# A hybrid attention, gating and retrieval layer on one core: all 128 chunks of one table turned during one projection

## The chip, the cores and the metric

The kernel runs on one core of one Trainium2 chip. The metric is the device time of one execution in microseconds (us), as the median of several runs. The profiled execution is another run of the same program, and its span runs from its first to its last instruction. In the rows below PE is the matrix engine, PEld its weight loads, DVE, ACT and POOL are the vector, scalar and GpSimd engines, and SP is the engine that here only issues transfers. A name with a q behind it (SPq, ACTq, POOLq) is the row of a transfer that this engine issued.

## What is computed

One layer of an encoder over 1024 tokens of width 1024, all in float32. The parts that matter here:

```python
h = rms_norm(x, g_pre_mix) * (1.0 + sc1) + sh1
p = h @ w_in                                  # the input projection, 56 column tiles of 128
q, k, v, z, gates = jnp.split(p, SPLITS, axis=-1)
o = diff_attention(q, k, v, lam)              # -> y_attn
sg = spatial_gating(jax.nn.gelu(z), ...)      # z = (u, v): u * mixed(layer_norm(v)) -> y_gmlp
gate_a, gate_g = jnp.split(jax.nn.sigmoid(gates), 2, axis=-1)
mix = (gate_a * y_attn + gate_g * y_gmlp) @ w_out
x = x + gt1 * rms_norm(mix, g_post_mix)
y = peer(rms_norm(x, g_pre_ffn) * (1.0 + sc2) + sh2, ...)

def peer(h, w_q, sub_keys, exp_u, exp_v):     # 16384 experts of one neuron each
    ...                                       # idx: for each token 8 heads x 16 experts
    u = exp_u[ib]
    a = jax.nn.gelu(jnp.einsum('td,ted->te', xb, u)) * gb
    return jnp.einsum('te,ted->td', a, exp_v[ib])
```

## The kernel before

The layer is a row of stages with a barrier of all engines between them. A matrix product is made of three products of rounded parts (`product3`: high by high, high by low, low by high), so that a tile of 128 output columns for 1024 tokens costs 48 matmuls of 128x512: two halves of the tokens, eight blocks of the inner dimension, three products each.

The method `projection` is the loop that several stages share. It goes over the column tiles of a weight. For each tile SP loads 512 KB of the weight (`raw`), ACT rounds it to the high part (L456), DVE makes the low part (L488), PE does the 48 matmuls (L382 to L384) into one of two accumulators, and the stage's own functions `act_out` and `dve_out` empty the accumulator. Weights and accumulators are double buffered.

Four stages matter:

- the **front** projection, 32 tiles of `w_in`, called in `gmlp_and_gates`. It has three stretches: 8 tiles of u (ACT applies gelu and stores 512 KB to `gelu_u_scratch`), 8 tiles of the other half of z (ACT applies gelu into SBUF, nothing is stored), and 16 tiles of gates (ACT applies the sigmoid and stores 512 KB to `gate_scratch`). In the gate tiles DVE also multiplies and sums pieces of the modulation matrix, and POOL loads 1024 KB of it for each tile (`gates_ada`, L1047), as soon as one of two buffers is free. The first two of the 16 pieces are loaded at the start of the stage.
- the **attn** and **spat** projections, 8 tiles each, with no row chunks;
- the **out** projection, 8 tiles of `w_out`, whose accumulator ACT squares (L1424) and copies (L1425), while DVE sums the squares.

Beside its own work a projection can turn **row chunks**. The table `peer_u` lies in memory with its inner dimension first, in 128 chunks of 128 experts. The last stage wants to fetch single experts as rows, so each chunk is loaded (512 KB), transposed by PE in eight 128x128 blocks, copied out of PSUM by ACT and stored as rows in `u_rows_scratch` (512 KB). How many chunks a tile turns, and from which chunk on, is the argument `rows=(per_tile, row_base)`. The chunks have two buffers on the way in (`r_in`), two in PSUM (`r_ps`) and two on the way out (`r_out`). The places in a tile come from `rows_at`: with three chunks they stand ahead of the 3rd, 9th and 14th of the 16 blocks of three matmuls, with four ahead of the 3rd, 7th, 11th and 15th. The three engines go like this:

```python
# SP, for each chunk n of tile j (after the weight of tile j + 2)
sp.wait_ge(r_turned, whole(n + 1))            # chunk n - 2 has been turned: r_in is free
sp.dma_start(r_in[:, slot], ... "peer_uT" ...).then_inc(r_loaded[slot], 16)
# PE, turn_rows
pe.wait_ge(r_loaded[slot], n * 8 + (16 - 8 * slot))
pe.wait_ge(r_copied, n + 1)                   # chunk n - 2 has left PSUM
for k in range(KT): last = pe.transpose(r_ps[slot][...], r_in[...], self.ident[:])
# ACT, empty, ahead of the tile's own output
act.wait_ge(r_turned, n + 3)
act.wait_ge(r_stored[slot], n * 8 + (16 - 8 * slot))   # chunk n - 2 has been stored
act.activation(r_out[:, slot], r_ps[slot], ACT.Copy).then_inc(r_copied, 1)
act.dma_start(self.u_rows[...], r_out[:, slot]).then_inc(r_stored[slot], 16)
```

All three engines work in order, so a chunk that is late holds what stands behind it on its engine. The first is L434 and L435, the second L550 to L554, the third L461 to L466. In the kernel before, the front projection turns three chunks per tile (96) and the out projection four (32).

Of the kernel before, what the change touches and what calls it, by code (L numbers as in the profile page):

```python
# [29 lines left out]
KT = D // P  # L30
# [23 lines left out]
Q0, K0, V0, ZU0, ZV0, GA0, GG0 = 0, 8, 16, 24, 32, 40, 48  # L54


class Layer:
# [925 lines left out]
    def gmlp_and_gates(self, h_hi, h_lo):  # L983
# [4 lines left out]
        nc, a, ps = self.nc, self.a, self.psum  # L988
        GATES = 2 * KT
        TILES = 2 * KT + GATES  # L990
# [9 lines left out]
        with ExitStack() as c:  # L1000
# [4 lines left out]
            with ExitStack() as p:  # L1005
                buf = self.sb(p, "front_buf", [P, 2, T])
                ada = self.sb(p, "gates_ada", [P, 2, 2, D])
                products = self.sb(p, "gates_products", [P, 2, 2, D])
                cb = self.sb(p, "gates_cb", [P, D])

                def to_scratch(func, dst, begin, made_before):

                    def act_out(act, j, s, acc, emptied):
                        own = j - begin

                        act.wait_ge(stored[s], (own + made_before) * 8 + (16 - 8 * s))
                        act.activation(buf[:, s], acc, func).then_inc(emptied, 1)

                        act.wait_ge(emptied, j + 3)
                        act.dma_start(dst[bass.ds(own, 1)].rearrange("o p t -> (o p) t"), buf[:, s]).then_inc(stored[s], 16)  # L1020
                    return act_out

                def zv_act_out(act, j, s, acc, emptied):
                    act.activation(zv[:, bass.ds(j - KT, 1)].rearrange("p o t -> p (o t)"), acc, ACT.Gelu_apprx_tanh).then_inc(emptied, 1)

                def zv_dve_out(dve, j, s, acc, emptied):

                    dve.wait_ge(emptied, j + 3)
                    dve.wait_ge(summed, j - KT + 1)
                    dve.tensor_tensor(total[:], total[:], zv[:, bass.ds(j - KT, 1)].rearrange("p o t -> p (o t)"), ALU.add).then_inc(summed, 1)  # L1030

                def gates_dve_out(dve, j, s, acc, emptied):
                    own = j - 2 * KT
                    dve.wait_ge(ada_loaded[s], own * 8 + (16 - 8 * s))

                    dve.wait_ge(dotted, own + 1)
                    dve.tensor_tensor(products[:, s], ada[:, s], cb[:].unsqueeze(1).to_broadcast([P, 2, D]), ALU.mult).then_inc(multiplied, 1)
                    dve.wait_ge(multiplied, own + 3)
                    dve.tensor_reduce(self.mod[:, bass.ds(own * 2 + MADE, 2)], products[:, s], AXX, ALU.add).then_inc(dotted, 1)

                def pool_program(pool, emptied):
                    with pool.Fori(0, GATES // 2) as it:
                        at = [pool.snap(it * 4 + (2 * s + MADE)) for s in range(2)]
                        for s in range(2):

                            pool.wait_ge(multiplied, it * 2 + (s + 1))
                            pool.dma_start(ada[:, s], a["w_adaT"][:, bass.ds(at[s], 2), :]).then_inc(ada_loaded[s], 16)  # L1047
                with nc.Block() as block:
                    @block.sync
                    def _(sp):  # L1050
                        sp.dma_start(cb[:], a["c"].to_broadcast([P, D])).then_inc(c_loaded, 16)
                        sp.dma_start(w[:].rearrange("q g p -> q (g p)"), a["w_spatial"]).then_inc(tables, 16)
                        sp.dma_start(bias[:].rearrange("q g p -> q (g p)"), a["b_spatial"].to_broadcast([P, KT * P])).then_inc(tables, 16)

                    @block.scalar
                    def _(act):
                        act.wait_ge(c_loaded, 16)
                        act.activation(cb[:], cb[:], ACT.Silu).then_inc(chain, 1)

                    @block.tensor  # L1060
                    def _(pe):
                        for s in range(2):
                            pe.sem_inc(stored[s], 16)

                    @block.vector
                    def _(dve):
                        dve.sem_inc(multiplied, 2)
                        dve.sem_inc(dotted, 2)
                        dve.memset(total[:], 0.0).then_inc(summed, 1)
                self.projection("front", a["w_in"], ZU0, h_hi, h_lo, TILES, pool_program=pool_program, rows=(3, 0), segments=[  # L1070
                    (0, KT, to_scratch(ACT.Gelu_apprx_tanh, self.u_scr, 0, 0), None),
                    (KT, 2 * KT, zv_act_out, zv_dve_out),
                    (2 * KT, TILES, to_scratch(ACT.Sigmoid, self.gate_scr, 2 * KT, KT), gates_dve_out)])
                with nc.Block() as block:
                    @block.sync
                    def _(sp):
                        for s in range(2):
                            sp.wait_ge(stored[s], 16 * ((KT + GATES) // 2 + 1))
# [335 lines left out]
    def out_projection(self, wide, m_hi, m_lo, total):  # L1414

        squared = self.sem("out_squared")
        summed = self.sem("out_summed")
        with ExitStack() as c:
            sq = self.sb(c, "out_sq", [P, 2, T])

            def act_out(act, j, s, acc, emptied):

                act.wait_ge(summed, j + 1)
                act.activation(sq[:, s], acc, ACT.Square).then_inc(squared, 1)  # L1424
                act.activation(wide[:, bass.ds(j, 1)].rearrange("p o t -> p (o t)"), acc, ACT.Copy).then_inc(emptied, 1)  # L1425

            def dve_out(dve, j, s, acc, emptied):
                dve.wait_ge(squared, j + 1)
                dve.wait_ge(summed, j + 2)
                dve.tensor_tensor(total[:], total[:], sq[:, s], ALU.add).then_inc(summed, 1)  # L1430
            with self.nc.Block() as block:
                @block.vector
                def _(dve):
                    dve.memset(total[:], 0.0).then_inc(summed, 1)
                    dve.sem_inc(summed, 1)
            self.projection("out", self.a["w_out"], 0, m_hi, m_lo, KT, act_out=act_out, dve_out=dve_out, rows=(4, 3 * 4 * KT))


    def add_normed(self, name, y, coef, base_dram, x1, dst_dram, total=None, squares_too=False):
# [1161 lines left out]
```

## Time and profile before

| | |
|---|---|
| median of 3 runs | 4668.48 us |
| lowest and highest run | 4663.53 and 4678.07 us |
| span of the profiled execution | 4674.6 us |
| PE busy | 3809.2 us, 81% of the span |
| DVE busy | 2888.6 us, 62% |
| ACT busy | 1496.4 us, 32% |
| POOL busy | 1266.7 us, 27% |
| read from and written to memory | 901.56 MB and 146.28 MB |

The stages follow each other with barriers, so what a change does in one stage shows in the length of that stage and moves all that follows. The shares of the whole span say little about a single stage. The front projection lasts from about 937 to 1397 us of the span, the out projection from about 1778 to 1903 us.

### The profile page before, as it was taken

To read this page: it belongs to the slowest core of one execution; us is meant where nothing else is said; L and a number is where in the kernel's file an instruction comes from. 1 tells how busy PE (TensorE), PEld (TensorE's weight loads), DVE (VectorE), ACT (ScalarE), POOL (GpSimd) and SP (SyncE) were. 2 spreads that over 40 slices of the span, in tenths; PEclk is the share of its full clock that TensorE was granted. 3 is DMA by queue.
4 is the path that set the end of the run, shared out by engine and by line. 5 is a ranking of instruction groups with operands and counts; after the bars stand their busy time and mean duration, and the time that the engine had idled before them with its cause. 6 is when DMAs were issued, how large, how long until landed. Compare 5 with 4: busy or idle time off the path is not lost. (4 is left out here: it accounts for less than half of the span.)

```text
span 4674.6 us, 50598 instructions
## 1 busy us (share of the span) xinstructions
PE 3809.2 (81%) x17580; PEld 2788.3 (60%) x17580; DVE 2888.6 (62%) x5552; ACT 1496.4 (32%) x2161; POOL 1266.7 (27%) x1080
## 2 busy tenths in 40 slices
PE   1889999699995898698666654389999999999996
PEld 1656666478775677587555543256666666665553
DVE  5666766401334431479677876877777777776665
ACT  3444444243433213411465561022222222221211
POOL 0000000000001000000000224667677767675442
PEclk9989999699995899699888877689999999999998
DMA  3000000087982226410245669899999999999996
GB/s 133 25 19 25 23 18 16 28 300 276 349 324 108 90 90 244 167 48 18 91 126 159 207 193 307 283 385 401 391 396 399 399 388 405 395 403 376 369 364 248
DMA packets 383399, 1050.26 MB, mean 225 GB/s; under 512 B 33264, under 2 KB 102256, under 8 KB 380016
## 3 DMA queue, kind: packets, MB, share of 16 engines
q0 software_dynamic: 153504, 567.35, 32.2%
q1 hardware_dynamic: 180960, 338.52, 21.1%
q10 hardware_dynamic: 48752, 142.10, 7.8%
q8 instruction: 96, 1.57, 0.1%
q14 instruction: 87, 0.71, 0.0%
HBM read 901.56 MB, written 146.28 MB: 224 GB/s over the span
## 5 line engine op out<-in xcount | busy, mean ns | idle before, releaser
L2280 POOL DMA_INDIRECT ex_v_rows<-peer_v_dram,expert_of x512 | 625.5, 1222 | 293.4 <-PE psum L2509 147.3
L2412 DVE TENSOR_TENSOR y<-y,psum 128x512 f32<-128x512 f32 x512 | 349.8, 683 | 379.8 <-PE psum L384 377.2
L382 PE MATMUL psum<-in_hi 128*128 128x512 f32 x1024 | 422.0, 412 | 67.0 <-ACT sc_gelu_t L2029 52.2
L2272 POOL DMA_INDIRECT ex_u_rows<-u_rows_scratch,expert_at x352 | 396.1, 1125 | 268.7 <-DVE dots L2405 176.7
L2405 DVE CUSTOM_DVE_ANT_1 ex_u_rows<-ex_u_rows,y 128x1024 f32<-128x1024 f32 x352 | 429.8, 1222 | 57.1 <-DMA ex_u_rows<-u_rows_scratch,expert_at 41.5
L382 PE MATMUL psum<-in_hi,v_hi 128*128 128x512 f32 x1024 | 430.6, 421 | 0.2 <-issue 0.2
L383 PE MATMUL psum<-in_lo,in_hi 128*128 128x512 f32 x1024 | 408.5, 399 | 0.0
L384 PE MATMUL psum<-in_hi,in_lo 128*128 128x512 f32 x1024 | 406.8, 397 | 0.0
L383 PE MATMUL psum<-in_lo,v_hi 128*128 128x512 f32 x1024 | 406.0, 396 | 0.0
L384 PE MATMUL psum<-in_hi,v_lo 128*128 128x512 f32 x1024 | 404.8, 395 | 0.0
L1047 POOL DMA_DIRECT2D gates_ada<-w_adaT_dram x16 | 8.7, 541 | 1363.2 <-PEq L532 931.4
L2509 PE MATMUL psum<-ex_v_rows,ex_spread 128*32 128x512 f32 x2048 | 283.3, 626 | 94.1 <-DMA ex_v_rows<-peer_v_dram,expert_of 93.0
L382 PEld LDWEIGHTS psum<-in_hi,v_hi 128*128 128x128 f32 x1024 | 194.9, 190 | 223.2 <-issue 125.0
L2130 PE MATMUL psum<-sc_first,sc_second 128*128 128x128 f32 x1024 | 169.3, 333 | 175.3 <-DVE sc_second L1957 175.3
L2323 ACT ACTIVATE in_hi<-g 128x512 fp32r<-128x512 f32 x128 | 80.8, 631 | 678.1 <-DVE g L2435 423.1
L382 PEld LDWEIGHTS psum<-in_hi 128*128 128x128 f32 x1024 | 198.7, 194 | 143.3 <-issue 91.3
L2130 PEld LDWEIGHTS psum<-sc_first,sc_second 128*128 128x128 f32 x1024 | 155.9, 240 | 205.3 <-DVE sc_second L1957 205.2
L384 PEld LDWEIGHTS psum<-in_hi,in_lo 128*128 128x128 f32 x1024 | 197.7, 193 | 43.6
L382 PE MATMUL psum<-in_hi,front_w_hi_t 128*128 128x512 f32 x512 | 209.5, 409 | 15.8 <-DVE front_w_lo_t L488 15.8
L384 PEld LDWEIGHTS psum<-in_hi,v_lo 128*128 128x128 f32 x1024 | 195.4, 191 | 44.3
L383 PEld LDWEIGHTS psum<-in_lo,in_hi 128*128 128x128 f32 x1024 | 198.6, 194 | 37.2
L383 PEld LDWEIGHTS psum<-in_lo,v_hi 128*128 128x128 f32 x1024 | 196.1, 191 | 33.5
(369 smaller groups left out, 8276.9 us busy)
## 6 DMA issues: line engine op xcount, KB each, us to landing
y<-peer_v_dram SPq DMA_DIRECT2D x128, 512.0 KB, 8.4
front_r_in<-peer_uT_dram SPq DMA_DIRECT2D x96, 512.0 KB, 4.8
u_rows_scratch<-front_r_out ACTq DMA_DIRECT2D x96, 512.0 KB, 5.3
route_scratch<-sc_stage SPq DMA_DIRECT2D x32, 1024.0 KB, 10.4
g<-route_scratch SPq DMA_DIRECT2D x128, 256.0 KB, 6.2
sc_u_raw<-peer_uT_dram SPq DMA_DIRECT2D x48, 512.0 KB, 4.8
y<-peer_uT_dram ACTq DMA_DIRECT2D x40, 512.0 KB
ex_u_next<-peer_uT_dram ACTq DMA_DIRECT2D x40, 512.0 KB
```

The costliest lines, as they stand in the source:

```text
L382: pe.matmul(out, w_hi, x_hi, start=start, stop=False)
L383: pe.matmul(out, w_hi, x_lo, start=False, stop=False)
L384: return pe.matmul(out, w_lo, x_hi, start=False, stop=stop)
L1047: pool.dma_start(ada[:, s], a["w_adaT"][:, bass.ds(at[s], 2), :]).then_inc(ada_loaded[s], 16)
L2130: last = pe.matmul(to, second[:, s, tok], first[:, s, tok], start=True, stop=True)
L2272: pool.indirect_dma_start(u_rows[:, r], None, every_u, bass.IndirectOffsetOnAxis(ap=expert_at[:, n // P, n % P:n % P + 1], axis=0)).then_i ...
L2280: pool.indirect_dma_start(v_rows[:, r * LANES + lane], None, every_v, bass.IndirectOffsetOnAxis(ap=expert_of[:, m // 32, t:t + 1], axis=0) ...
L2323: act.activation(act_hi[ring], g[:, s], ACT.Copy).then_inc(a_hi_done, 1)
L2405: dve.tensor_tensor_reduce(out=halves(u_rows[:, r]), in0=halves(u_rows[:, r]), in1=rows, scale=1.0, scalar=0.0, op0=ALU.mult, op1=ALU.add, ...
L2412: dve.tensor_tensor(to, to, ps[:, n % 4], ALU.add).then_inc(added, 1)
L2509: last = pe.matmul(ps[lane * 32:(lane + 1) * 32, 4 + half], spread[:, first:first + 32], v_rows[:, r * LANES + lane, half * HALF:(half + 1 ...
```

## The change

The front projection turns four chunks per tile instead of three, which makes all 128; the out projection turns none. The number of transposes, copies, loads and stores is the same; 32 chunks move from one stage to another that runs some 400 us earlier.

```diff
-                self.projection("front", a["w_in"], ZU0, h_hi, h_lo, TILES, pool_program=pool_program, rows=(3, 0), segments=[
+                self.projection("front", a["w_in"], ZU0, h_hi, h_lo, TILES, pool_program=pool_program, rows=(4, 0), segments=[
...
-            self.projection("out", self.a["w_out"], 0, m_hi, m_lo, KT, act_out=act_out, dve_out=dve_out, rows=(4, 3 * 4 * KT))
+            self.projection("out", self.a["w_out"], 0, m_hi, m_lo, KT, act_out=act_out, dve_out=dve_out)
```

On SP, in the loop of the front projection, a piece of the difference; ISA rows are waits on semaphores, REGISTER_ALU rows work out a semaphore's target:

```order
 L435 ISA
 L435 DMA front_r_in<-peer_uT_dram 128x1024
+L434 REGISTER_ALU
+L435 ISA
+L435 DMA front_r_in<-peer_uT_dram 128x1024
 L428 REGISTER_ALU
 L429 ISA
```

A fourth load stands at the end of a tile's chunks, ahead of the load of a later weight (L429).

On ACT in the same loop, ahead of the tile's own output (from L1016 on):

```order
 L466 ISA
 L466 DMA u_rows_scratch<-front_r_out 128x1024
+L461 REGISTER_ALU
+L463 ISA
+L464 ACTIVATE front_r_out<-psum 128x1024
+L466 ISA
+L466 DMA u_rows_scratch<-front_r_out 128x1024
 L468 REGISTER_ALU
 L1016 ISA
```

A fourth copy and a fourth store, each behind a wait, now come ahead of the tile's sigmoid or gelu.

On PE in the out projection:

```order
 L383 MATMUL psum<-in_lo,out_w_hi_t 128x512
 L384 MATMUL psum<-in_hi,out_w_lo_t 128x512
-L550 ISA
-L552 REGISTER_ALU
-L554 MATMUL psum<-ident,out_r_in 128x128 x8
```

The waits and the eight transposes are gone, here and at every other chunk of that stage, and the matmuls follow each other.

## Rows read from the trace of the kernel before

**Rows 1.** Windows: stretch, length, busy us per engine, clock (1.00 is 2.4 GHz), DMA share, GB/s.

```profile
core 0: us, PE busy (x) PEld busy (x) DVE busy (x) ACT busy (x) POOL busy (x), PEclk, DMA share, GB/s
937.00:1053.00 116.00, 110.82 (x570) 93.09 (x571) 10.29 (x9) 48.74 (x47) 0.00 (x0) 0.95 0.85 300
1053.00:1162.00 109.00, 109.00 (x578) 92.10 (x577) 17.75 (x15) 40.53 (x41) 0.00 (x0) 1.00 0.80 277
1178.00:1280.00 102.00, 96.97 (x507) 80.06 (x505) 40.61 (x22) 44.00 (x42) 3.70 (x7) 1.00 0.96 354
1280.00:1395.00 115.00, 108.44 (x568) 89.73 (x568) 43.82 (x23) 47.52 (x45) 3.70 (x7) 1.00 0.92 338
1778.00:1903.00 125.00, 119.86 (x640) 100.30 (x640) 17.29 (x15) 52.44 (x54) 0.00 (x0) 0.97 0.82 291
4000.00:4200.00 200.00, 192.15 (x914) 130.59 (x913) 153.98 (x234) 43.47 (x58) 139.63 (x117) 0.99 1.03 404
```

**Rows 2.** Timeline of PE around one chunk: start us, us, engine, line, operation, tiles.

```profile
1091.49 0.39 PE L384 MATMUL psum<-in_hi,front_w_lo_t 128*128 128x512 f32 x1
...
1092.17 0.40 PE L384 MATMUL psum<-in_hi,front_w_lo_t 128*128 128x512 f32 x1
1092.41 1.04 PE L554 MATMUL psum<-ident,front_r_in 128*128 128x128 f32 x8
1093.20 0.47 PE L382 MATMUL psum<-in_hi,front_w_hi_t 128*128 128x512 f32 x1
1093.51 0.39 PE L383 MATMUL psum<-in_lo,front_w_hi_t 128*128 128x512 f32 x1
```

**Rows 3.** Timeline of ACT: the end of front tiles 8, 15, 16 and 31.

```profile
1068.45 1.03 ACT L1024 ACTIVATE zv<-psum 128x1024 f32 x1 [1.07 <-PE psum L384]
...
1163.71 1.03 ACT L1024 ACTIVATE zv<-psum 128x1024 f32 x1 [1.04 <-PE psum L384]
1177.30 1.28 ACT L1017 ACT_TABLE_LOAD   x1 [1.04 <-PE psum L384]
...
1395.97 1.02 ACT L1017 ACTIVATE front_buf<-psum 128x1024 f32<-128x1024 f32 x1 [1.06 <-PE psum L384]
```

**Rows 4.** Waits, 1162 to 1397 us: who waited for whom, total us, times, longest.

```profile
ACT front_r_out L464 <- DMA u_rows_scratch<-front_r_out: 69.7, 14, 6.7
...
PE psum L554 <- DMA front_r_in<-peer_uT_dram: 11.5, 11, 1.8
...
PEld psum L554 <- ACT front_r_out L464: 2.2, 1, 2.2
```

**Rows 5.** Transfers issued, 1165 to 1395 us: count, KB each, median us to landing.

```profile
u_rows_scratch<-front_r_out ACTq DMA_DIRECT2D x48, 512.0 KB, 6.7
front_r_in<-peer_uT_dram SPq DMA_DIRECT2D x46, 512.0 KB, 5.9
gates_ada<-w_adaT_dram POOLq DMA_DIRECT2D x14, 1024.0 KB, 8.4
gate_scratch<-front_buf ACTq DMA_DIRECT2D x15, 512.0 KB, 5.3
front_w_raw<-w_in_dram SPq DMA_DIRECT2D x13, 512.0 KB, 7.9
```

**Rows 6.** Timeline of PE: first and last matmul of spat, then of out.

```profile
1674.55 0.79 PE L382 MATMUL psum<-sg_hi,spat_w_hi_t 128*128 128x512 f32 x1 [9.00 <-DVE spat_w_lo_t L488]
...
1763.83 0.39 PE L384 MATMUL psum<-sg_hi,spat_w_lo_t 128*128 128x512 f32 x1
1778.27 0.79 PE L382 MATMUL psum<-in_hi,out_w_hi_t 128*128 128x512 f32 x1 [14.05 <-DVE out_w_lo_t L488]
...
1784.65 1.38 PE L554 MATMUL psum<-ident,out_r_in 128*128 128x128 f32 x8 [3.46 <-DMA out_r_in<-peer_uT_dram]
...
1901.57 0.39 PE L384 MATMUL psum<-in_hi,out_w_lo_t 128*128 128x512 f32 x1
```

**Rows 7.** Timeline of all engines at the end of out.

```profile
1901.67 0.34 ACTq L466 DMA_DIRECT2D u_rows_scratch<-out_r_out  x1
1902.11 1.02 ACT L1424 ACTIVATE out_sq<-psum 128x1024 f32<-128x1024 f32 x1 [0.47 <-PE psum L384]
1903.03 1.02 ACT L1425 ACTIVATE mixed<-psum 128x1024 f32<-128x1024 f32 x1
1903.22 1.23 DVE L1430 TENSOR_TENSOR out_total<-out_total,out_sq 128x1024 f32<-128x1024 f32 x1 [13.29 <-ACT out_sq L1424]
1905.61 0.38 SPq L1454 DMA_DIRECT2D x<-xT_dram  x1
```

## The prediction

> **What bounds the kernel now.** I first cut the span into the stretches of the two stages that the change touches and read engines, clock and transfers in each [rows 1]. In the first 16 front tiles, and in out, PE is busy nearly all the time: 109.00 of 109.00 us in the second stretch of front, where the transfers take 0.80 of the DMA engines' time. There PE is the bound. The 16 gate tiles are different: the DMA share is 0.96 and 0.92, PE idles 5.0 us of 102 and 6.6 of 115, and the clock stays at 1.00, so the idle time is not clock. The waits of that stretch say what PE lacks: the load of a chunk (11.5 us) and the copy of one (2.2 us); ACT in turn waits 69.7 us for stores of earlier chunks [rows 4]. So the gate tiles already stand at the edge of what the transfers give, and the other stages do not.
>
> The paces say the same. Tiles 8 to 15 end 13.61 us apart ((1163.71 - 1068.45) / 7). Tile 16 takes 13.59, then tiles 17 to 31 take 14.58 on average ((1395.97 - 1177.30) / 15), though PE has the same work [rows 3]. Tiles 17 to 30 have a load of 1024 KB beside them, 14 of them in the stretch, landing in a median of 8.4 us [rows 5]. If tile 31, which has none, takes 13.6, those 14 take 14.65 each. The whole gate stretch, from the end of tile 15 to that of tile 31, lasts 232.3 us.
>
> **What a chunk costs PE.** Three matmuls start 0.68 us apart (1091.49 to 1092.17), 0.227 each. From the L384 ahead of a chunk to the L383 behind it are 1.34 us (1092.17 to 1093.51), where two steps of 0.227 would be 0.45 [rows 2]. A chunk therefore costs PE 0.89 us where data is there in time.
>
> **Part 1, out loses 32 chunks: a gain of 34.0 us.** I don't add this up from parts, since the trace has the stage without chunks: spat, with the same 8 tiles and 384 matmuls of the same shape. From its first to its last matmul it takes 89.28 us, out takes 123.30 [rows 6]. The difference, 34.0 us, holds 28.4 us for 32 chunks, 3.46 us of waiting for the first chunk at 1784.65 and some 2.2 us of small waits. Both begin at the low clock, with matmuls of 0.63 to 0.79 us, so that is in both. What is late next in out without chunks: ACT's split, square and copy, some 3 us of work per tile, DVE's subtraction and sum, 2.5 us, and one weight of 512 KB, all beside 10.9 us of matmuls. The same chain hides in spat. Behind the last matmul come square and sum on ACT and DVE [rows 7]; they stay. The last chunk's store was issued at 1901.67 and the next stage's first transfer follows the end of DVE's sum (1904.45) by 1.2 us, so I take nothing more from the store's going: between 0 and 0.5 us.
>
> **Part 2, the first 16 front tiles get a fourth chunk: a loss of 20.4 us.** On PE 8 x 0.89 = 7.1 us in each stretch. The rest is waiting, which the first two stretches don't show now. In tiles 8 to 15 a tile will move 9 x 512 KB (weight, four loads, four stores), 4.72 MB in 14.50 us, 325 GB/s. Out moves just that today, at a cost of the 2.2 us above over 8 tiles: I take 2.2. In the u tiles a store comes on top: 5.24 MB in 14.50 us, 362 GB/s. That is what an ada tile moves now (10 x 512 KB in 14.65 us, 358 GB/s) at 1 us of wait per tile. But there a large load on another queue shares the engines for 8.4 of those 14.65 us [rows 5], and out waited little at 0.82 of the DMA engines [rows 1], so I take the middle of 0 and 1.0: 0.5 us a tile, 4 us. The sum is 7.1 + 4.0 + 7.1 + 2.2 = 20.4 us, with ends of 14.2 and 26. The first chunk's wait at the start of front stays as it is: `rows_at` puts it ahead of the 3rd block as before.
>
> **Part 3, the gate tiles get a fourth chunk: a loss of 35.4 us.** Were PE the bound, this would cost 14.2 us. But an ada tile would then have to move 12 x 512 KB, 6.29 MB, in 15.5 us: 405 GB/s. At 0.96 of the engines' time this mix makes 354 GB/s, which is 369 at a full share [rows 1]. By 369, an ada tile takes 17.05 us; two tiles without ada take 14.50. The stretch is 14 x 17.05 + 2 x 14.50 = 267.7 us, 35.4 more than now. The tile's time is then set by bytes and not by PE: the fourth chunk's 1.05 MB costs 2.4 us a tile, of which PE's 0.89 is hidden. The order of waits is: the load of a chunk is late, PE stands ahead of its eight transposes with the tile's remaining matmuls behind them; and ACT stands ahead of its copy until a store has landed, with the tile's sigmoid and the split of a later weight behind it. The split has a whole tile of slack, PE's place has none. Bounds: at the 404 GB/s of the expert stage [rows 1] an ada tile takes 15.57 us and the loss is 14.7 us; at 354, with nothing gained from a fuller queue, 17.8 us and 45.5 us. I stay near the row of the same stretch, since it is the same mix of loads and stores, and the other is mostly loads.
>
> SP gets no later for anything but this: its fourth load waits for the second chunk of its tile to be turned, and the weight queued behind it is for two tiles ahead. POOL's loads are paced by DVE, whose gate work comes once a tile. DVE and ACT have spare time (40.6 and 44.0 us busy in 102). The later stages read `u_rows_scratch` hundreds of us later and see no difference.
>
> **The sum.** 20.4 + 35.4 - 34.0 = +21.8 us. The profiled span of 4674.6 us would become 4696.4. That execution lies 6.1 us above the median of the runs, 4668.5, so the median becomes 4690.3; I forecast **4690 us**. Below, "about the same" means within 0.3% (14 us), about what a measurement of this kernel can tell from no change.
>
> **Rivals.**
>
> *The transfers keep up.* If four chunks fill the queues better and the mix reaches the 404 GB/s that the expert stage holds for 200 us, Part 3 costs 14.7 us, Part 2 only its 14.2 on PE, and the sum is -5.1 us: 4663 us, not slower. For it: in the gate tiles the share is below 1, and the loads come in bursts. Against it: PE is already held up at 354. It decides from 395 GB/s on, the rate at which an ada tile takes 15.94 us and the sum is zero.
>
> *The mix has no more to give than it makes now.* At 354 GB/s the sum is 20.4 + 45.5 - 34.0 = +31.9: 4700 us. For it: tiles that wait already make no more than this. Against it: the expert stage's 404, and the share of 0.96. The Trainium skill, page "DMA: Bandwidth & Descriptors", section "Specifications", gives a limit of about 358 GB/s that a core gets from memory; by it an ada tile would take an estimated 17.6 us and the sum would be +29 us. The expert stage's 404 GB/s over 200 us speaks against it as a limit here, while the gate tiles' own rate fits it.
>
> *The stores' way round becomes the bound.* A chunk's `r_out` buffer is taken for a copy (1.03), an issue (0.34) and the landing; with two buffers a chunk can pass every half of that. At today's median landing of 6.7 us [rows 5] that is 4.0 us a chunk, 16.1 us a tile, hidden behind 17. If landings rise to 8 us, it is 4.7 and 18.7, the stretch lasts 290.8 us and the sum is +44.9: 4713 us. For it: ACT's 69.7 us of waiting. Against it: with two stores under way, a landing grows just because bytes are short, and these are counted already.
>
> **How the numbers follow.** The forecast's own case, a rate between 360 and 385 GB/s in the gate tiles, gets 0.60 and reaches from 4675 to 4700. The transfers keep up: 0.16. Nothing more than 354: 0.14. The stores' way: 0.07. A gain that I see no mechanism for: 0.03. Slower by over 0.3% means above 4682.5: about 0.47 of the first case and both slow rivals, 0.68. Within 0.3%: 0.13 of the first case and nearly all of the fast rival, 0.28. Faster: 0.04. The range of 4665 to 4708 leaves out the ends of the fast rival and of the slowest one.
>
> **What would show it.** In the profile of the changed kernel: out from first to last matmul in some 89 us; tiles 8 to 15 about 14.8 us apart; ada tiles about 17 us apart, with a DMA share near 1.0 and PE's waits for chunk loads risen from 11.5 to some 35 us, at a clock of still 1.00. Ada tiles at 15.5 us would make it wrong towards no change; a clock that falls in longer waits, or chunks spaced by landings, would make it wrong upward.

## The result: 0.86% slower, and the profile after

The changed kernel takes 4714.31 us in the median (4704.26 to 4720.39), the kernel before 4673.27 us in the same comparison. The ratio is 1.0086, with a 95% interval from 1.0067 to 1.0106: slower, as forecast, by 41 us and not by 22. The measured time lies above the range of the prediction. The profiled execution has a span of 4718.7 us, 44.1 more than that of the kernel before.

The windows of the changed kernel, over the three stretches of front and over out, with the columns of [rows 1]:

```profile
core 0: us, PE busy (x) PEld busy (x) DVE busy (x) ACT busy (x) POOL busy (x), PEclk, DMA share, GB/s
941.00:1075.00 134.00, 120.91 (x643) 99.88 (x641) 8.58 (x7) 56.48 (x54) 0.00 (x0) 0.96 0.91 320
1075.00:1192.00 117.00, 116.28 (x638) 98.09 (x639) 17.75 (x15) 48.71 (x49) 0.00 (x0) 1.00 0.92 325
...
1210.00:1330.00 120.00, 103.47 (x526) 84.89 (x524) 36.37 (x20) 47.52 (x45) 3.18 (x6) 0.94 0.95 342
1330.00:1475.00 145.00, 124.98 (x654) 102.60 (x654) 45.04 (x24) 57.81 (x55) 3.71 (x7) 0.96 0.94 339
1855.00:1946.00 91.00, 88.94 (x384) 73.05 (x383) 17.49 (x15) 21.20 (x22) 0.00 (x0) 0.98 0.11 35
```

The gate tiles have more to move than before, and the rate did not rise: it is 342 and 339 GB/s, against 354 and 338 in [rows 1]. PE idles 16.5 us of 120 and 20 of 145, and its clock is 0.94 and 0.96 there, not 1.00.

The ends of tiles 7, 15, 16, 30 and 31 in ACT's timeline of the changed kernel, which answer to [rows 3]:

```profile
1076.46 1.03 ACT L1017 ACTIVATE front_buf<-psum 128x1024 f32<-128x1024 f32 x1 [0.68 <-ACT front_r_out L464]
...
1192.45 1.02 ACT L1024 ACTIVATE zv<-psum 128x1024 f32 x1 [0.71 <-ACT front_r_out L464]
...
1207.06 1.28 ACT L1017 ACT_TABLE_LOAD   x1 [0.68 <-ACT front_r_out L464]
...
1460.14 1.03 ACT L1017 ACTIVATE front_buf<-psum 128x1024 f32<-128x1024 f32 x1 [0.47 <-PE psum L384]
...
1475.01 1.02 ACT L1017 ACTIVATE front_buf<-psum 128x1024 f32<-128x1024 f32 x1 [0.47 <-PE psum L384]
```

Tiles 8 to 15 are 14.50 us apart ((1192.45 - 1076.46) / 8), the 14 gate tiles with a modulation load 18.08 ((1460.14 - 1207.06) / 14). The waits of the gate stretch (1192 to 1476 us), to set beside [rows 4]:

```profile
ACT front_r_out L464 <- DMA u_rows_scratch<-front_r_out: 118.0, 28, 8.4
...
PE psum L554 <- DMA front_r_in<-peer_uT_dram: 36.3, 19, 3.8
...
PEld psum L554 <- ACT front_r_out L464: 4.1, 2, 3.8
```

The last row adds no idle time to the one above it. Its 3.8 us are one of PE's waits for a load, seen from the weight loads:

```profile
1440.98 0.85 PEld L554 LDWEIGHTS psum<-ident,front_r_in 128*128 128x128 f32 x8 [3.82 <-ACT front_r_out L464]
1440.99 1.09 PE L554 MATMUL psum<-ident,front_r_in 128*128 128x128 f32 x8 [3.40 <-DMA front_r_in<-peer_uT_dram]
```

PE's timeline around the longest wait shows what the clock does behind it, here on PE's own matmuls:

```profile
1412.56 0.39 PE L384 MATMUL psum<-in_hi,front_w_lo_t 128*128 128x512 f32 x1
1416.77 1.96 PE L554 MATMUL psum<-ident,front_r_in 128*128 128x128 f32 x8 [3.83 <-DMA front_r_in<-peer_uT_dram]
1418.38 0.78 PE L382 MATMUL psum<-in_hi,front_w_hi_t 128*128 128x512 f32 x1
1418.96 0.63 PE L383 MATMUL psum<-in_lo,front_w_hi_t 128*128 128x512 f32 x1
```

After 3.83 us of waiting the transposes take 1.96 us where they took 1.04 in [rows 2], and the matmuls 0.63 instead of 0.39: PE runs at 1.2 GHz for some microseconds. The window from 1415 to 1422 us has a granted clock of 0.51. Not every long wait is followed by this: behind the 3.40 us at 1440.99 the transposes took 1.09 us.

Out, from first to last matmul, to set beside [rows 6]:

```profile
1854.56 0.79 PE L382 MATMUL psum<-in_hi,out_w_hi_t 128*128 128x512 f32 x1 [13.91 <-DVE out_w_lo_t L488]
...
1943.56 0.39 PE L384 MATMUL psum<-in_hi,out_w_lo_t 128*128 128x512 f32 x1
```

That is 89.00 us, 34.3 less than before.

For the first stretch the trace of the kernel before has a start and an end that were not shown yet, the first matmul of front and the end of tile 7:

```profile
937.62 0.79 PE L382 MATMUL psum<-in_hi,front_w_hi_t 128*128 128x512 f32 x1 [15.79 <-DVE front_w_lo_t L488]
...
1054.80 1.03 ACT L1017 ACTIVATE front_buf<-psum 128x1024 f32<-128x1024 f32 x1 [1.01 <-PE psum L384]
```

In the changed kernel the first matmul comes at 939.18. The 44.1 us of the two spans divide as follows:

| stretch | before | after | difference | forecast |
|---|---|---|---|---|
| up to front's first matmul | 937.6 | 939.2 | +1.6 | 0 |
| front, tiles 0 to 7 (u) | 117.2 | 137.3 | +20.1 | +11.1 |
| front, tiles 8 to 15 | 108.9 | 116.0 | +7.1 | +9.3 |
| front, tiles 16 to 31 (gates) | 232.3 | 282.6 | +50.3 | +35.4 |
| from there to out's first matmul | 382.3 | 379.6 | -2.7 | 0 |
| out, first to last matmul | 123.3 | 89.0 | -34.3 | -34.0 |
| the rest | 2773.0 | 2775.1 | +2.1 | 0 |

The bounds inside front are ACT's, and ACT can lag behind PE. In the changed kernel it empties tile 7 only 5.1 us after PE has begun tile 8. PE begins tiles 8 and 16, before and after, at:

```profile
1054.52 0.39 PE L382 MATMUL psum<-in_hi,front_w_hi_t 128*128 128x512 f32 x1
...
1163.40 0.39 PE L382 MATMUL psum<-in_hi,front_w_hi_t 128*128 128x512 f32 x1
```

```profile
1071.34 0.40 PE L382 MATMUL psum<-in_hi,front_w_hi_t 128*128 128x512 f32 x1
...
1191.10 0.39 PE L382 MATMUL psum<-in_hi,front_w_hi_t 128*128 128x512 f32 x1
```

By these the u tiles lost 15.3 us and tiles 8 to 15 10.9; only the two together, 26 to 27 us, are sharp.

The gain came in as forecast; the loss in front was 77.5 us and not 55.8. The question for the experiments was what holds the gate tiles, and the u tiles, at 320 to 345 GB/s.

### The profile page after: what moved, and what is told of

Read it like the earlier page. It is cut to its first block and busy times, and to the rows that moved or that the text cites. A ratio compares the mean times of both kernels' runs of the same rounds, so it can differ in the third digit from the quotient of the medians.

```text
span 4718.7 us, 50628 instructions
## 1 busy us (share of the span) xinstructions
PE 3828.5 (81%) x17580; PEld 2797.3 (59%) x17580; DVE 2887.6 (61%) x5552; ACT 1495.9 (32%) x2161; POOL 1266.7 (27%) x1080
## 5 line engine op out<-in xcount | busy, mean ns | idle before, releaser
L382 PE MATMUL psum<-in_hi,front_w_hi_t 128*128 128x512 f32 x512 | 216.0, 422 | 15.3 <-DVE front_w_lo_t L488 15.3
L464 ACT ACTIVATE front_r_out<-psum 128x1024 f32<-128x1024 f32 x128 | 131.2, 1025 | 269.0 <-DMA u_rows_scratch<-front_r_out 191.0
```

The source lines that it names most:

```text
L382: pe.matmul(out, w_hi, x_hi, start=start, stop=False)
```

## The experiments

Two theories stood at the start. By **bytes**, the DMA engines move this mix of loads and stores at about 345 GB/s and not faster; that was the prediction's own step, with 369. By **rings**, the engines could move more, but a chunk has two buffers on each way, and a load is issued only when the chunk two places ahead has been turned: the pace is set by landing times. The kernels with deeper rings have other line numbers: L475 is ACT's copy and L566 PE's transposes there.

### Four buffers on the way in alone

```diff
+            DI, DO = per_tile, 2
...
-                r_in = self.sb(c, f"{name}_r_in", [P, 2, D])
+                r_in = self.sb(c, f"{name}_r_in", [P, DI, D])
...
-                            act.wait_ge(r_turned, n + 3)
+                            act.wait_ge(r_turned, n + (1 + DI))
```

The semaphores of the loads become as many as the buffers, and `r_turned` starts at that number, so that SP's wait lets a load go when the chunk four places ahead has been turned.

> The changed kernel with four buffers instead of two for chunks on the way in (r_in), two on the way out as before. In the changed kernel the u tiles end 16.2 us apart, the gate tiles with a modulation load 18.1 us apart, and PE waits 40 us for chunks in the gate stretch. Theory BYTES (the engines move this mix of loads and stores at no more than about 345 GB/s, whatever is queued): all stays, u tiles 16.2, gate tiles 18.1, within 0.3. Theory LOADS (a chunk's load is issued only when the chunk two places ahead has been turned, so 6.4 us ahead of its use, and its landing takes as long): PE waits for loads nearly vanish, u tiles 14.6, gate tiles 16.5. Theory STORES (the way out holds the copies and through them PE): PE stalls move from the load to the copy, tiles stay within 0.4.

Measured: 4700.42 us in a single run, beside 4675.32 for the kernel before. The gate stretch fell from 282.6 to 268.8 us, the gate tiles to 17.27; the u tiles rose to 16.73. The waits of the gate stretch (1193 to 1462 us) are:

```profile
ACT front_r_out L475 <- DMA u_rows_scratch<-front_r_out: 124.5, 42, 6.4
...
PE psum L566 <- ACT front_r_out L475: 24.4, 24, 2.0
...
PE psum L566 <- DMA front_r_in<-peer_uT_dram: 5.7, 6, 1.3
```

PE's wait for loads has fallen from 36.3 to 5.7 us, and 24.4 us have come back as a wait for ACT's copy, which waits for a store. Neither BYTES (the rate rose to 362 and 351 GB/s) nor LOADS (16.5 us for the gate tiles) is right by itself. STORES had the moved wait right, but both kinds of tile changed by more than its 0.4 us.

### Four buffers on the way out alone

The same edit for `r_out` and its semaphores, with `DI, DO = 2, per_tile`.

> The changed kernel with four buffers instead of two for chunks on the way out (r_out), two on the way in as before. BYTES: u tiles 16.2, gate tiles 18.1, as now. LOADS: the same as now, since the loads are what PE waits for (36 of 40 us). STORES: ACT's waits for stores, 118 us in the gate stretch, go, and the tiles shorten to 14.6 and 16.5.

Measured: 4719.7 us in a single run. The u tiles fell to 15.29 us, the gate tiles rose to 18.53. ACT's waits for stores are gone, and PE waits for loads (1200 to 1480 us):

```profile
ACT front_r_out L475 <- PE psum L566: 151.0, 48, 6.7
...
PE psum L566 <- DMA front_r_in<-peer_uT_dram: 40.3, 23, 3.2
```

ACT now waits for PE, and PE for loads, as LOADS had said, which had left the u tiles unchanged too; they fell by 0.9 us. So whichever way is left with two buffers holds the chunks.

### Four buffers on both ways

Both edits together, `DI, DO = per_tile, per_tile`, and one buffer instead of two for DVE's products of the modulation pieces.

> The changed kernel with four buffers on both ways (and one buffer less for the products of the modulation pieces, which DVE orders anyway). BYTES: within 5 us of the changed kernel, some 1.008 of the kernel before. LOADS: as with four buffers on the way in alone. STORES: as with four on the way out alone. If both ways hold it in turn: only this one shortens it, u tiles 14.6, gate tiles 16.5, and the whole lies near the kernel before, 0.998 to 1.003.

Measured: 4651.73 us beside 4675.32, a ratio of 0.9955 (0.9940 to 0.9971). The u tiles are 14.52 us apart, the gate tiles 14.92, and the gate stretch lasts 237.9 us: more was gained than the last case expected, with its 16.5 and 0.998 to 1.003. Two windows of the gate tiles:

```profile
1193.00:1300.00 107.00, 105.39 (x575) 88.12 (x574) 43.20 (x24) 54.52 (x52) 4.23 (x8) 1.00 1.02 413
1300.00:1400.00 100.00, 97.83 (x537) 81.95 (x536) 35.16 (x19) 46.49 (x45) 3.17 (x6) 1.00 1.02 420
```

The same loads and stores now run at 413 and 420 GB/s, and the clock is back at 1.00. BYTES has fallen: there was no ceiling at 345, nor at 369. The transfers issued between 1193 and 1400 us (count, KB each, median us to landing):

```profile
u_rows_scratch<-front_r_out ACTq DMA_DIRECT2D x56, 512.0 KB, 8.3
front_r_in<-peer_uT_dram SPq DMA_DIRECT2D x56, 512.0 KB, 11.6
gates_ada<-w_adaT_dram POOLq DMA_DIRECT2D x14, 1024.0 KB, 9.2
```

In the changed kernel with two buffers, from 1192 to 1476 us, it was:

```profile
u_rows_scratch<-front_r_out ACTq DMA_DIRECT2D x65, 512.0 KB, 5.9
front_r_in<-peer_uT_dram SPq DMA_DIRECT2D x62, 512.0 KB, 6.4
```

Landings got longer, 11.6 us for a load instead of 6.4, and PE hardly waits (3.7 us for loads in the whole gate stretch). A load now has up to four chunks' time to land. With two it had about 6.4 us at PE's own pace (two intervals of 3.63 less the transposes), which is the very median of its landing. PE waited ahead of 19 of the 64 chunks.

The whole gate stretch in the kernel before, in the changed kernel and in this one, with the columns of [rows 1]:

```profile
1163.70:1396.00 232.30, 220.64 (x1152) 182.26 (x1150) 87.39 (x47) 98.59 (x94) 7.39 (x14) 1.00 0.93 340
```

```profile
1192.40:1475.00 282.60, 245.87 (x1275) 202.06 (x1273) 87.58 (x47) 115.01 (x109) 7.42 (x14) 0.96 0.94 339
```

```profile
1177.00:1414.90 237.90, 234.01 (x1279) 195.88 (x1277) 86.97 (x47) 114.98 (x109) 7.40 (x14) 1.00 0.98 399
```

The last two have the same matmuls and transposes. Deeper rings took 32.8 us from PE's idle time (36.7 to 3.9) and 11.9 us from its busy time; that is what the lower clock had cost.

A rival is the order on SP, which issues the load of a later weight ahead of a tile's chunk loads. In the gate stretch of the changed kernel (1192 to 1476 us) this held nothing back, since SP waited for turned chunks alone:

```profile
SPq L435 <- PE psum L554: 230.0, 62, 7.2
```

### The kernel before with deeper rings

Three buffers each way in front and four in out, chunks as before.

> The kernel before with as many buffers each way as chunks per tile (three in the front, four in the out projection), nothing else changed. BYTES: the gate stretch stays at 232 us and the time within 0.2%. LOADS or both ways: the 14 us that PE waits in the gate stretch mostly go (stretch 220 us), and some 2 us in out: 0.996 to 0.998.

Measured: 4663.78 us beside 4675.32, 0.9980 (0.9969 to 0.9990), at the upper end of what the rings theory expected. The gate stretch fell from 232.3 to 227.2 us, where 220 was expected, and out stayed at 123.4, where 2 us less were expected. The waits of PE and of SP in the gate stretch (1163 to 1391 us; L438 is the load of a weight):

```profile
PE psum L566 <- DMA front_r_in<-peer_uT_dram: 7.5, 10, 1.4
```

```profile
SPq L438 <- DVE front_w_lo_t L499: 94.5, 13, 7.6
```

Three buffers take away about a third of the 11.5 us that PE waited with two. For the other two thirds the order on SP is the cause: the weight's load waits for the split of an earlier weight, and the chunk loads stand behind it. A kernel further down (also three chunks a tile, but the chunk loads ahead of the weight) differs from this one by that order and by the single buffer for DVE's products; its gate stretch is 217.7 us, and PE does not wait in it.

### One part of the change alone

```diff
-                self.projection("front", a["w_in"], ..., rows=(3, 0), segments=[
+                self.projection("front", a["w_in"], ..., rows=(4, 0), segments=[
```

> One part of the change alone: the front projection turns four chunks per tile, and the out projection turns its 32 again, as before, so that these are turned twice. If the two parts of the change add up as the two traces say: front gets 77.5 us longer as in the changed kernel, out stays at 123.3 us from first to last matmul, and the time is some 75 us above the kernel before, 1.016. If the shorter out stage of the changed kernel had given something back elsewhere, less.

Measured: 4741.87 us beside 4677.61, 1.0141 (1.0124 to 1.0158), +64 us. Some 75 us were expected, so the whole came out 11 us short. By its trace front is 74.5 us longer and out takes 124.0 us, both near what was expected. The time between them is 375.7 us, 6.6 less than in the trace of the kernel before, and the time behind out 6.1 less. The stages there have no part in the change. From front to out the eleven traces of these runs have 371.5 to 382.3 us, with a clock of 0.63 to 0.68 over the first 168 us in eight of them, and behind out 2765.6 to 2784.0 us. I have no run that settles why. A sum over a whole single trace is therefore uncertain by some 10 us; the lengths of front and of out repeat better.

### Without the modulation loads

```diff
-                    with pool.Fori(0, GATES // 2) as it:
...
-                            pool.wait_ge(multiplied, it * 2 + (s + 1))
-                            pool.dma_start(ada[:, s], a["w_adaT"][:, bass.ds(at[s], 2), :]).then_inc(ada_loaded[s], 16)
+                    for s in range(2):
+                        pool.dma_start(ada[:, s], a["w_adaT"][:, 2 * s + MADE:2 * s + MADE + 2, :]).then_inc(ada_loaded[s], 16)
```

> The changed kernel without 14 of the 16 loads of modulation pieces (DVE multiplies the first two again and again; the modulation is then not that of the reference). In the gate tiles the transfers are then those of the u tiles: one weight, four chunk loads, four chunk stores, one output store. Theory RINGS (with two buffers each way the pace is set by the landing times, and any further transfer lengthens these): the gate tiles take what the u tiles take, 16.2 us, not the 14.5 of PE, at some 325 GB/s; the clock falls in fewer waits than now. Theory POOL QUEUE (the large load on the third queue is what holds the chunks): gate tiles fall to 14.5.

Measured: 4672.25 us in a single run, beside 4677.61. The gate tiles are 15.54 us apart, the u tiles 15.95 in the same run. Two windows of the gate tiles:

```profile
1210.00:1330.00 120.00, 113.08 (x616) 93.52 (x615) 41.85 (x22) 54.24 (x52) 0.00 (x0) 1.00 0.95 332
1330.00:1440.00 110.00, 102.86 (x561) 85.61 (x559) 41.70 (x22) 51.04 (x49) 0.00 (x0) 1.00 0.91 327
```

At 332 and 327 GB/s, well below what the engines gave with four buffers, the tiles still miss PE's 14.5 by 1.0 us. That lies between the two theories, nearer to RINGS. The POOL queue's load is therefore not what holds the chunks by itself. It costs 18.08 - 15.54 = 2.5 us a tile: without it chunk loads land in 4.8 us in the median instead of 6.4 and chunk stores in 5.4 instead of 5.9, and the clock stays at 1.00.

### Chunk loads ahead of the weight

With four buffers each way, the order of SP in the loop is turned round:

```diff
-                            weights(it * 2 + (2 + s), s)
                             row_chunks(it * 2 + s, s)
+                            weights(it * 2 + (2 + s), s)
```

> The changed kernel with four buffers each way (as deep_both), and on SP the four chunk loads of a tile ahead of the load of a later weight instead of behind it. Rings with four buffers keep the pace of 14.5 us in u tiles and 14.9 in gate tiles either way. PE's wait for the first chunk, 4.6 us at the start of the stage, goes, since the first loads no longer wait for the split of the first weight, and with it some of the start at the low clock: 4 to 7 us below deep_both, 0.994 of the kernel before. If the rings need the weight ahead of the chunks, weights come late and the tiles get longer.

Measured: 4641.86 us beside 4677.61, 0.9928 (0.9911 to 0.9944). The start of front in this kernel, SP's loads and PE's first chunk (L438 is a weight, L445 a chunk):

```profile
931.97 0.80 SPq L438 DMA_DIRECT2D front_w_raw<-w_in_dram  x2
...
933.55 3.04 SPq L445 DMA_DIRECT2D front_r_in<-peer_uT_dram  x4
...
943.23 1.96 PE L566 MATMUL psum<-ident,front_r_in 128*128 128x128 f32 x8
```

The wait ahead of the first chunk, 4.5 us with the weight first, is gone, and the u stretch took 119.8 us instead of 124.4. But the first matmul came at 940.26 instead of 936.42, so that the u tiles end only 0.8 us earlier. The eight kernels here with the weight first begin between 936.4 and 940.7, so this doesn't show that the order delays the first matmul. Nor is a gain over four buffers alone shown: the ratio is 0.9928 here, 0.9950 when the same kernel ran again (below), and was 0.9955 there.

### Is the move worth anything once the rings are deep?

> The kernel before (three chunks per front tile, four per out tile) with the two edits of deep_first: as many buffers each way as chunks per tile, and the chunk loads ahead of the later weight. It differs from deep_first only by the move of 32 chunks. Theory: with deep rings a chunk costs PE 0.89 us wherever it stands, so the move is worth nothing: the same time as deep_first within 0.3%, front and out together 560 us from first to last matmul in both (front 441, out 119, against 471 and 89), about 0.993 of the kernel before. Rival: the gate tiles still lose to the transfers with four chunks, so that this one is 5 us or more faster than deep_first.

> deep_first once more, beside the run above on the same chip, for a comparison of the two: 0.993 of the kernel before, as then.

Measured on one chip: 4648.64 us with 32 chunks in out, 4648.54 with all in front, beside 4668.57 for the kernel before (0.9952 and 0.9950, where 0.993 had been expected for both). Each is the median of four runs that spread over 15 to 17 us. The windows of the first, then of the second, over the stretches of front and over out:

```profile
940.00:1054.00 114.00, 112.67 (x578) 94.61 (x579) 9.77 (x8) 49.07 (x47) 0.00 (x0) 0.96 0.88 307
1054.00:1163.00 109.00, 109.00 (x578) 92.07 (x577) 17.75 (x15) 40.54 (x41) 0.00 (x0) 1.00 0.81 276
1163.00:1381.00 218.00, 217.51 (x1151) 183.35 (x1150) 87.36 (x47) 98.94 (x94) 7.40 (x14) 1.00 0.96 363
1757.00:1875.00 118.00, 117.82 (x640) 99.75 (x640) 17.20 (x15) 51.50 (x53) 0.00 (x0) 0.98 0.86 302
```

```profile
939.00:1058.00 119.00, 118.53 (x643) 100.06 (x644) 9.53 (x8) 57.38 (x55) 0.00 (x0) 0.98 1.00 367
1058.00:1174.00 116.00, 116.00 (x641) 98.42 (x640) 17.75 (x15) 48.51 (x48) 0.00 (x0) 1.00 0.92 331
1174.00:1410.00 236.00, 232.93 (x1279) 196.16 (x1277) 87.74 (x47) 115.86 (x110) 7.39 (x14) 1.00 1.00 404
1783.00:1875.00 92.00, 89.14 (x384) 73.36 (x384) 18.38 (x15) 21.66 (x23) 0.00 (x0) 0.97 0.11 37
```

From first matmul to the last in each stage these are 558 us in front and out together for the first and 559 for the second. PE is busy nearly throughout in both. The change moves work that costs PE the same at either place; its 41 us were the price of two-deep rings. Deeper rings are enough to take that price away: with the weight still first, the kernel with 32 chunks in out took 4663.78 us and the one with all in front, which has one buffer less for the products, 4651.73, so that there the move gained 12 us. The first also shows that three buffers each way are enough for three chunks where the loads go ahead of the weight: its gate stretch takes 217.7 us, 13.6 a tile, which is PE's own pace.

## Why the prediction was wrong

The direction, the place and the term for out held. The term for the first 16 tiles came out at or above its upper end, and the largest term was mis-sized because its mechanism was wrong.

**A chunk's cost on PE, 0.89 us: right.** With four buffers, where PE doesn't wait in them, tiles 8 to 15 are 14.52 us apart instead of 13.61. The 14.50 of the changed kernel come near only because ACT's lag is in the bounds; by PE's starts it is 14.97.

**Part 1, out: right.** Forecast -34.0, measured -34.3. Taking the length from another stage without chunks did better than adding durations would have, since the first chunk's wait was in it.

**Part 3, the gate tiles: the step that failed.** It said that the mix makes 354 GB/s at 0.96 of the engines' time, 369 at a full share, and that bytes set the tile's time: 17.05 us a tile and 35.4 us in all. It took 18.08 us a tile and 50.3 in all, at 342 and 339 GB/s. The engines were not the bound: with four buffers they moved the same mix at 413 to 420. The DMA share of 0.96 in [rows 1] was read as nearness to a limit. But 0.96 stood beside 363 GB/s without waits in the last run but one, and 0.95 beside 332 with waits in the run without modulation loads. Even the gate tiles of the kernel before, which "already stand at the edge of what the transfers give", go at PE's pace with the same chunks in that last run but one. What set the pace was the rings: with four chunks a tile, a load has 6.4 us from its issue to its use where it had 8, against landings of 5.9 us in the median [rows 5]. That could have been worked out from the rows that were there.

By the windows of the whole stretch, the 50.3 us are 25.1 more of PE's idle time (36.7 against 11.7), 13.4 for the transposes (PE's busy time at a clock of 1.00, 234.0 against 220.6) and 11.9 of clock, which the prediction left at 1.00 and so put at nothing. The prediction named both as signs that it would be wrong upward: "a clock that falls in longer waits, or chunks spaced by landings". It also counted 2.2 us of waiting for a copy beside the 11.5 for loads; PE's idle time of 5.0 and 6.6 us in [rows 1] has room for the loads alone.

**Part 2, the first 16 tiles: right in kind, wrong in size.** By ACT's bounds the u tiles cost 20.1 and not 11.1 us, tiles 8 to 15 7.1 and not 9.3; by PE's starts 15.3 and 10.9, so that both lie above the forecast. The middle that I took between no wait and 1 us a tile was too low for the u tiles (16.2 us apart against PE's 14.5); in the other eight PE waited 2.8 us for loads, where 2.2 had been taken from out. The two stretches differ by one store of 512 KB a tile on ACT's queue. Chunk loads land in a median of 5.7 us in the u tiles and 4.8 in the other eight, chunk stores in 5.7 and 5.3. That fits the rings, but no run took the store away alone. With four buffers each way the u stretch is 124.4 us, 7.2 above the kernel before: what was lost beyond PE's transposes was the rings' here too.

**The rivals.** The time came out near that of the third rival, the stores' way round (4713 us), but that is luck: its condition was that landings of stores rise to 8 us, and they fell from 6.7 to 5.9. Its mechanism is half of the true one: with two buffers the way out holds, but so does the way in, and freeing either alone moved much of the wait to the other. The rival in which transfers keep up named a rate that this mix can reach, but not the condition for it, which is deeper rings. The Trainium skill's limit of about 358 GB/s for a core (page "DMA: Bandwidth & Descriptors", section "Specifications") is there a stack's 716 GB/s halved for two cores. With one core at work it did not bind: the gate tiles with four buffers ran at 413 to 420.

**SP.** "The first chunk's wait at the start of front stays as it is" held for this change, but the wait was no given: it came from the order of two lines on SP.

## What to carry to other kernels

Before adding transfers to a pipeline, compare for each ring the time from a transfer's issue to its use with the landing time in the trace, at the new spacing; where the two are close, the ring and not the bandwidth can be the bound, as here, and a busy share of the DMA engines near 1 does not show otherwise. Deepen both directions of a load, work and store chain together, since freeing one can move the wait to the other, and see that no load on the same engine's queue stands waiting ahead of them. Work that costs an engine the same in two stages is worth moving only if one of the two stages makes that engine wait.

## What was not expected of the hardware

A core moved 413 to 420 GB/s over 200 us, with seven bytes loaded for every five stored, while the same mix with two buffers each way stood at 342 GB/s with the DMA engines shown as busy 0.95 of the time: the share says little about how much more fits. And some waits ahead of a chunk were followed by a stretch at half the clock (3.83 us of waiting, then a granted clock of 0.51 over 7 us), so that waiting cost more than its own length: 11.9 us in the gate stretch beside 36.7 of idle time. In the kernel before, the longest wait there was 1.8 us and the clock stayed at 1.00.
